# Value rows fetched in turn with key rows inside the GLA recurrences, and narrow products side by side in four lanes, in an fp32 two-layer decoder step

## What is computed

```python
for li in range(DEPTH):                                       # DEPTH = 2
    mod = silu(c) @ ada_w[li] + ada_b[li]                     # 9 rows, 6 kinds of 1024 columns
    sh1, sc1, gt1, sh2, sc2, gt2 = split(mod, 6)
    hm = rmsnorm(x, norm1_g[li]) * (1 + sc1) + sh1
    out, S = rwkv7_mix(hm, ...) if li % 2 == 0 else gla_mix(hm, ...)
    x = x + gt1 * out
    hc = rmsnorm(x, norm2_g[li]) * (1 + sc2) + sh2
    x = x + gt2 * peer(hc, wq[li], subkeys[li], u[li], v[li])

def peer(x, wq, subkeys, u, v):
    # 8 heads, 16 of 128 x 128 experts each by product keys: 128 experts for every token
    expert, gate = top16_of_pairs(x @ wq, subkeys)
    act = gelu(einsum('thed,td->the', u[expert], x))          # key rows: 128 dot products a token
    return einsum('the,thed->td', gate * act, v[expert])      # value rows, weighted
```

## Time and profile before

| | |
|---|---|
| runs of the kernel | 3150.2, 3168.51, 3175.33 us; median 3168.51 |
| the profiled execution | 3167.07 us, its span in the trace 3165.2 us |
| mean granted clock of TensorE | 0.764 of full speed |
| PE busy | 1890.7 us (60 %) |
| DVE busy | 1640.9 us (52 %) |
| POOL busy | 1284.7 us (41 %) |
| PE weight loads | 1084.3 us (34 %, beside PE) |
| ACT busy | 266.3 us (8 %) |
| DMA | 827.99 MB, mean 262 GB/s |

### The profile page before, as it was taken

How to read it: one execution, slowest core, us unless ns; L and a number is a source line. 1 busy time by engine, 2 the same in 40 slices (tenths; PEclk the granted TensorE clock), 3 DMA queues, 4 the chain that set the end, 5 groups by cost and what they waited for, 6 DMA issues and landing times.

```text
span 3165.2 us, 24264 instructions
## 1 busy us (share of the span) xinstructions
PE 1890.7 (60%) x8947; PEld 1084.3 (34%) x8947; DVE 1640.9 (52%) x3013; ACT 266.3 (8%) x421; POOL 1284.7 (41%) x1160
## 2 busy tenths in 40 slices
PE   4889777836947554545684765766346954002537
PEld 1459422326825123333252325343243810000103
DVE  3253375574935437859413226866873262784033
ACT  0111000110100100000100100001110000000000
POOL 0000002452614554535322444466530255777773
PEclk8889888966878776657787877878567967556668
DMA  7530576963858885757887889798775588999996
GB/s 241 175 112 12 194 269 208 344 221 106 269 203 292 331 294 194 243 167 228 286 307 282 307 281 328 249 341 312 225 242 190 218 282 306 380 361 384 409 409 263
DMA packets 296705, 827.99 MB, mean 262 GB/s; under 512 B 45950, under 2 KB 57134, under 8 KB 296588
## 3 DMA queue, kind: packets, MB, share of 16 engines
q0 software_dynamic: 165888, 604.05, 53.1%
q1 hardware_dynamic: 120132, 218.02, 19.9%
q10 hardware_dynamic: 10568, 4.38, 0.5%
HBM read 816.05 MB, written 10.31 MB: 261 GB/s over the span
## 4 chain that ended last, share of the span: by engine, by line
PE 33%; DVE 23%; DMA 19%; POOL 13%; issue 7%; ACT 2%; PEld 1%; SPq 1%; ACTq 0%; DVEq 0%; PEldq 0%; POOLq 0%
PE psum L1750 31%; POOL arena L613 13%; DMA arena<-in_peer_v,idx_v 7%; DVE arena L973 7%; DVE arena L956 7%; DMA wring<-in_gla_w_in 2%; DMA wring<-in_rw_w_rkv 2%; DMA vring<-mod_d 2%; DMA wring<-in_ada_w 1%; DMA wring<-in_peer_wq 1%; DVE hc L956 1%; PE psum L1760 1%; DMA out<-arena 1%; DVE hT L956 1%; PEld psum L1750 1%
## 5 line engine op out<-in xcount | busy, mean ns | idle before, releaser
L1750 PE MATMUL psum<-arena 128*32 128x512 f32 (+6 forms) x4066 | 839.6, 623 | 620.4 <-DMA arena<-in_peer_v,idx_v 279.6
L613 POOL DMA_INDIRECT arena<-in_peer_u,idx_u x576 | 719.5, 1249 | 1094.5 <-DVE acts L973 503.1
L973 DVE CUSTOM_DVE_ANT_0 arena<-arena,hc 128x1024 f32<-128x1024 f32 x576 | 688.7, 1224 | 288.4 <-DMA arena<-in_peer_u,idx_u 219.8
L613 POOL DMA_INDIRECT arena<-in_peer_v,idx_v x512 | 498.8, 974 | 705.0 <-PE psum L1750 551.6
L1750 PEld LDWEIGHTS psum<-arena 128*128 128x128 f32 (+2 forms) x4066 | 399.7, 179 | 1007.9 <-issue 723.7
L1750 PE MATMUL psum<-hT,wring 128*128 128x128 f32 (+3 forms) x1824 | 233.3, 290 | 12.1 <-ACT arena L654 6.3
L1750 PEld LDWEIGHTS psum<-hT,wring 128*128 128x128 f32 (+1 forms) x1824 | 222.0, 195 | 34.8 <-issue 17.1
L1750 PE MATMUL psum<-wring,hT 128*128 128x512 f32 (+1 forms) x480 | 191.7, 559 | 25.1 <-DMA wring<-in_gla_w_in 13.3
L654 ACT ACTIVATE arena<-psum 128x512 f32<-128x512 f32 (+5 forms) x142 | 108.1, 761 | 1131.0 <-PE psum L1750 923.9
L1750 PE MATMUL psum<-wring,cT 128*9 128x512 f32 x384 | 178.1, 622 | 23.0 <-DMA wring<-in_ada_w 16.1
L1750 PE MATMUL psum<-wring,arena 128*128 128x512 f32 (+2 forms) x408 | 157.4, 543 | 26.6 <-DMA wring<-in_rw_w_rkv 13.3
(11 more groups left out here) (207 smaller groups left out, 1564.8 us busy)
## 6 DMA issues: line engine op xcount, KB each, us to landing
wring<-in_ada_w SPq DMA_DIRECT2D x24, 2048.0 KB
wring<-in_peer_wq SPq DMA_DIRECT2D x20, 2048.0 KB
wring<-in_rw_w_rkv SPq DMA_DIRECT2D x12, 2048.0 KB
wring<-in_gla_w_in SPq DMA_DIRECT2D x12, 2048.0 KB
wring<-in_rw_wo SPq DMA_DIRECT2D x6, 2048.0 KB
vring<-mod_d SPq DMA_DIRECT2D x22, 512.0 KB
arena<-in_peer_u,idx_u POOLq DMA_INDIRECT x576, 6.2
arena<-in_peer_v,idx_v POOLq DMA_INDIRECT x512, 6.3
```

Source lines behind the costliest of these rows:

```text
L613: pool.indirect_dma_start(slots[s], None, v_rows if side else u_rows, bass.IndirectOffsetOnAxis(index, 0)).then_inc(rows_landed[s], 16)
L973: dve.tensor_tensor_reduce(slots[s], slots[s], hc[:, t, :], 1.0, 0.0, MUL, ADD, acts[:, (3 * li + t) % 2, col:col + 1]).then_inc(rows_used ...
L1750: return nc.tensor.matmul(out, lhsT, rhs, start=start, stop=stop)
```

## The change

Three parts.

1. **Mingled rounds.** For the one pair in `MINGLED`, layer 2's tile 0, the second half of the key rounds (16 to 31) and the first half of the value rounds (0 to 15) alternate, in `round_at` as in POOL's issue order: one group of the ring then holds key rows, the other value rows. POOL waits for `experts_dealt` after the first key round of the second half. PE opens 16 value rounds ahead of the recurrences of tiles 1 and 2 with a rate of 0.6, multiplies what is left of them behind (`rest_values`), and opens the other 16 where all 32 were opened. On both engines these streams are `paired`: they are served at PSUM results that DVE takes (`for_vector`, `fill`) and at no other wait. DVE's rate goes from 1.6 to 2.4.
2. **The sample tile's values in lanes.** Each of the four slots of a round gets a 32-column product into its own 32 partitions, as for the prompt tiles. One diagonal build takes the place of four. Before the sum is used, DVE copies `total` to SBUF and PE adds the four lanes by a product with `rep32` (`sum_lanes`); this stands once ahead of layer 2's first mixer and once at the end.
3. **Modulations in lanes.** `cT` gets 32 columns for each block (zeros behind the nine), and the eight blocks go to four lanes, two into each. ACT copies the lanes' parts out of PSUM over the first two blocks of the second weight buffer, and PE sums the lanes by a product with nine columns of `rep32`. That buffer is released after this sum.

```diff
--- before.py
+++ after.py
...
-def span_of(t):
-    return 8 if t == SAMPLE else 32
+def spans_of(t):
+    return fetches_of(t) // FOLD
+def spans_ahead(li, t):
+    return sum(spans_of(u) for u in (0, 1, SAMPLE)) * li + sum(spans_of(u) for u in range(t))
+MINGLED = ((1, 0),)
...
     each = fetches_of(t) // GRP
-    return li * 2 * (2 * P + SHORT) // GRP + t * 2 * P // GRP + side * each + r
+    at = side * each + r
+    if (li, t) in MINGLED:
+        first = each // 2
+        if side == 0 and r >= first:
+            at = first + 2 * (r - first)
+        elif side and r < first:
+            at = first + 2 * r + 1
+    return li * 2 * (2 * P + SHORT) // GRP + t * 2 * P // GRP + at
...
     def __init__(self):
-        self.credit, self.rate, self.left = 0.0, 0.0, 0
-    def open(self, count, rate):
+        self.credit, self.rate, self.left, self.paired = 0.0, 0.0, 0, False
+    def open(self, count, rate, paired=False):
...
         self.credit = 0.0
-    def due(self, work):
+        self.paired = paired
+    def due(self, work, product):
+        if self.paired and not product:
+            return 0
...
-        bias_slot, pack_buffer = {}, {}
+        bias_slot, parts_buffer, pack_buffer = {}, {}, {}
+        def parts_of(b):
+            return wring[:, b, 0:2, :].rearrange("p k n -> p (k n)")
...
                 for j in range(2 * k, 2 * k + 2):
-                    weight(a["ada_w"][li][:, j * 512:(j + 1) * 512])
+                    parts_buffer[li, k] = weight(a["ada_w"][li][:, j * 512:(j + 1) * 512])
...
                     rounds = fetches_of(t) // GRP
+                    mingled = (li, t) in MINGLED
...
                         gather(li, t, 0, r)
-                    if t < SAMPLE:
+                        if mingled and r >= rounds // 2:
+                            if r == rounds // 2:
+                                pool.wait_ge(experts_dealt, w.next(experts_dealt))
+                            gather(li, t, 1, r - rounds // 2)
+                    if t < SAMPLE and not mingled:
                         pool.wait_ge(experts_dealt, w.next(experts_dealt))
-                    for r in range(rounds):
+                    for r in range(rounds // 2 if mingled else 0, rounds):
...
                 copy_out(HT(t), D)
+            def copy_parts(li, k):
+                copy_out(parts_of(parts_buffer[li, k]), D)
+                act.sem_inc(parts_copied, 1)
+            def copy_early_parts(li, k):
+                act.wait_ge(mods_parted, w.next(mods_parted))
+                done(act.activation(parts_of(parts_buffer[li, k]), total, ACT.Copy))
+                act.sem_inc(parts_copied, 1)
...
                 root(s16[:, 0, :])
+                for li, k in PREP_MODS[t]:
+                    copy_parts(li, k)
...
                 for li, k in END_MODS[t]:
+                    copy_parts(li, k)
+                for li, k in END_MODS[t]:
...
                     for m in (CHOOSE_MODS[2 * half:2 * half + 2] if first else ()):
+                        copy_early_parts(*m)
...
                 if first:
+                    copy_early_parts(*CHOOSE_MODS[4])
...
             act.sem_inc(operand_written, 1)
-            copy_out(cT[:, :], KD * 9)
+            copy_out(cT[:, :].rearrange("p (k n) -> p k n", k=KD)[:, :, 0:9], KD * 9)
...
             copy_out(muT[:, :], 48)
+            for k in range(2):
+                copy_parts(0, k)
...
             stream = Share()
-            RATES = {"mix": 14, "core1": 1.9, "core2": 2.6, "enter": 6, "gla": 1.6, "out": 7}
+            RATES = {"mix": 14, "core1": 1.9, "core2": 2.6, "enter": 6, "gla": 2.4, "out": 7}
...
-            def open_rows(li, t, first, count, rate):
+            def open_rows(li, t, first, count, rate, paired=False):
                 at[:] = li, t, first
-                stream.open(count, rate)
-            def serve(work=1.0):
-                for _ in range(stream.due(work)):
+                stream.open(count, rate, paired)
+            def serve(work=1.0, product=False):
+                for _ in range(stream.due(work, product)):
...
             def fill():
-                serve()
+                serve(1.0, True)
...
                     dve.wait_ge(total_ready, phase)
-                span = span_of(t)
-                m = D // span
+                span, m = FOLD, D // FOLD
                 src = (acts if t == SAMPLE else wf)[:, phase % 2, :]
-                for q in (range(4) if t == SAMPLE else (2 * half, 2 * half + 1)):
+                for q in ((0,) if t == SAMPLE else (2 * half, 2 * half + 1)):
...
                 dve.wait_ge(total_ready, 3 * li + t + 1)
+                if t == SAMPLE:
+                    done(dve.tensor_copy(tmp, total))
+                    dve.sem_inc(lanes_copied, 1)
+                    dve.wait_ge(lanes_summed, w.next(lanes_summed))
...
                     weights_due(1, 0, 0)
-                    open_rows(1, 0, 64, 64, RATES["gla"])
+                    open_rows(1, 0, 64, 64, RATES["gla"], True)
...
             at = [0, 0, 0]
-            VALUE_RATES = {"out": 0.5, "gla": 0.5}
+            VALUE_RATES = {"out": 0.5, "gla": 0.5, "mingled": 0.6, "core2": 0.8}
...
                 at[2] += 1
-                phase, span, rounds = 3 * li + t, span_of(t), fetches_of(t) // GRP
+                phase, span, rounds = 3 * li + t, FOLD, fetches_of(t) // GRP
...
                 if r * GRP % span == 0:
-                    pe.wait_ge(diag_ready, 4 * phase + chunk + 1)
+                    pe.wait_ge(diag_ready, spans_ahead(li, t) + chunk + 1)
...
                     for j in range(GRP):
-                        lane = slice(0, P) if t == SAMPLE else slice(m * j, m * j + m)
-                        start = r == 0 and (j == 0 or t != SAMPLE)
-                        stop = r == rounds - 1 and (j == GRP - 1 or t != SAMPLE)
+                        lane = slice(m * j, m * j + m)
+                        start, stop = r == 0, r == rounds - 1
...
-            def open_values(li, t, rate):
-                at[:] = li, t, 0
-                stream.open(fetches_of(t) // GRP, rate)
+            def sum_lanes():
+                pe.wait_ge(lanes_copied, w.next(lanes_copied))
+                for h in range(2):
+                    last = mm(total[:, h * 512:(h + 1) * 512], rep32[:], add_tmp[:, h * 512:(h + 1) * 512])
+                last.then_inc(lanes_summed, 1)
+            def open_values(li, t, rate, count=None, first=0, paired=False):
+                at[:] = li, t, first
+                stream.open(fetches_of(t) // GRP if count is None else count, rate, paired)
...
-            def serve(work=1.0):
-                for _ in range(stream.due(work)):
+            def serve(work=1.0, product=False):
+                for _ in range(stream.due(work, product)):
...
             def for_vector():
-                serve()
+                serve(1.0, True)
...
-            def modulation():
-                ps = for_vector()
+            def mod_parts(dst):
...
                     for kk in range(KD):
-                        last = mm(ps[0:9, j * 512:(j + 1) * 512], cT[:, kk * 9:(kk + 1) * 9], wring[:, b, kk, :], kk == 0, kk == KD - 1)
+                        g = FOLD * (kk % COPIES)
+                        last = mm(dst[g:g + FOLD, j * 512:(j + 1) * 512], cT[:, kk * FOLD:(kk + 1) * FOLD],
+                                  wring[:, b, kk, :], kk < COPIES, kk >= COPIES)
...
                         last.then_inc(weight_used[b], 1)
-                    else:
-                        last.then_inc(psum_for_vector, 1)
-                        release(b, psum_for_vector, nfv[0])
+                return last, b
+            def mod_sum(dst, b):
+                pe.wait_ge(parts_copied, w.next(parts_copied))
+                for j in range(2):
+                    last = mm(dst[0:9, j * 512:(j + 1) * 512], rep32[:, 0:9], parts_of(b)[:, j * 512:(j + 1) * 512])
+                return last
+            def modulation():
+                last, b = mod_parts(for_scalar())
+                last.then_inc(psum_for_scalar, 1)
+                mod_sum(for_vector(), b).then_inc(psum_for_vector, 1)
+                release(b, psum_for_vector, nfv[0])
...
                     pe.wait_ge(mods_taken, n)
-                for j in range(2):
-                    b = weight()
-                    for kk in range(KD):
-                        last = mm(total[0:9, j * 512:(j + 1) * 512], cT[:, kk * 9:(kk + 1) * 9], wring[:, b, kk, :], kk == 0, kk == KD - 1)
-                    if j == 0:
-                        last.then_inc(weight_used[b], 1)
-                    else:
-                        last.then_inc(mods_summed, 1)
-                        release(b, mods_summed, n + 1)
+                last, b = mod_parts(total)
+                last.then_inc(mods_parted, 1)
+                mod_sum(total, b).then_inc(mods_summed, 1)
+                release(b, mods_summed, n + 1)
...
+                if tiles[0]:
+                    sum_lanes()
...
```

(5 more changed lines are left out.)

8 lines of the change are left out of this document (7 added, 1 removed).

## The result

The changed kernel takes 3115.01 us (median of four runs, 3103.15 to 3122.44) against 3167.65 us for the kernel before: the ratio is 0.9848, with a 95 % interval of 0.9813 to 0.9884. The forecast was 3101 us. The profiled execution took 3103.15 us with a span of 3101.3 us, so the trace shows a gain of 63.9 us of span where the medians show 52.6: it is the quickest of the four.

The account below looks back on a forecast made before the run. No engine was taken to bound the kernel: a chain of stages in series. 3165.2 less 21 (mingled rounds), 16 (sample lanes) and 29 (modulations), plus 0.5, gave 3099.7, so 3101 us; range 3065 to 3145 for 8 in 10.

Parts of the forecast that it names:

- the second rival: Lower clock and loads: PE's short modulation bursts run at 3.64 us, that part is worth 12, time 3118 us; chance 0.14.
- 65 us of growth: Recurrences of layer 2's tiles 1 and 2: 16 added value rounds lengthen them by 65 us.
- 86.5 us of the stages behind: Behind the recurrences: sample tile's choice ends at 2618.5, so next key products start 86.5 us sooner than at 2705.0.
- The ten distances: Ten of fifteen distances between mingled value rounds, paced by a slot group's trip of 14.2 us: 142 us together.
- the five longer ones: Five distances between mingled value rounds set by the recurrence's own work: 85.9 us now, 91.4 with the added rounds.
- its floor: Mingled value rounds: a group's trip (slots freed, gathers issued, landing, round) of 14.2 us is their least distance.
- S: What the recurrences of layer 2's tiles 1 and 2 grow by: 65 us taken, about 45 to 100 as bounds.
- The price of POOL's issue: Gathers in the recurrences: 1.32 us each and some 0.3 between them, adding 1.2 us to a group's trip.
- land the last 5.7 us later: Sample tile's end: after POOL issues the 16 gathers left in 19 us, the last value rows land 5.7 us later.
- the 35 to 38 of the sign: Sign of being right: the sample tile's last eight value rounds take 35 to 38 us.
- Three places: Modulations at the start, ahead of the first recurrence and in the first choice: gains of 7, 7.4 and 10 us.
- the 5 us taken there: Modulations at the sample tile's end, paced by two loads at once: gain between 3 and 7.5 us, 5 taken.

Follow-up runs that it names:

- the kernel without a way out: The whole change, but modulations leave out ACT's copy and PE's sum, so only the first lane's blocks reach the result: ratio 0.9829 to the kernel before.

## Why the prediction was right, and where its terms were off

**The range and the sign** held: 3115 lies in 3065 to 3145, and all three parts gain. The forecast's own band, 3088 to 3112, was missed by 3 us. The time is nearer to the second rival's 3118 than to 3101, but by another sum: that rival took 17 us from the modulations alone, while the runs take 5 to 7 us from each of the three parts.

**Mingled rounds: the sizes right, by a mechanism that holds where the value side is last.** Forecast were 65 us of growth and 86.5 us of the stages behind; measured 63 to 69, and 79 to 81. The second was short by the second deal: the prediction let PE's rounds end long ahead of it, but with PE at 3.3 us a round and 6.4 to 7.3 us from start to start the last ends at 2622.4, and the deal comes 6 to 8 us sooner instead of 13.6.

The first can be taken apart in the change's trace. The ten distances that the prediction set at 142 us together take 144.2, the five longer ones, set at 91.4, take 86.6. Eight of the ten are closed trips of 13.9 us for the 14.2, with parts that were off against each other: from the first to the fourth issue 3.9 us for 4.9, from there to PE's start 6.4 for 5.7, the round 3.4 for 3.64. Value rounds do have a pace of their own, and the rates don't set it: 15.4 us on average, and 15.3 with rates a quarter higher. What the prediction lacks is how close the key side stands behind: shortening the trip frees 13 us where its floor would free 20 or 26, and fewer value rounds free 0 to 8. That S came within 2 us is in part luck: the ten distances came out 2 us longer and the five 5 us shorter.

The price of POOL's issue was the part read too high. It came from a window in which DVE was full; in the same 69 us of the changed stage POOL is busy 39.5 us for 35 gathers, 1.13 each where the earlier trace rows had 1.32, and DVE is idle a third of the time.

```profile
2158.37:2227.37 69.00, 26.70 (x132) 13.38 (x136) 45.27 (x77) 10.36 (x19) 39.45 (x35) 0.60 0.74 251
```

**Sample tile's lanes: the term was mis-sized, 9 us for 16.** The step that failed is "land the last 5.7 us later": that landing came from a stretch with a short queue. At the end four gathers of 128 rows take 5.1 us because the DMA is full, and the rounds wait for them: from the last issue to PE's start it is 12.8 us, 7.1 more than the 5.7, and POOL, which waits for the rounds, issues its last gather 4 us later than the sum had it. The queue was noticed and given 5 us; it cost 11.4 more than the first sum, and the rounds take 43.0 us, not the 35 to 38 of the sign. Copy and sum were right: 5.2 for 4.6. In layer 1 the builds win 4.1 to 4.3 us and the way from there to the sum's use loses 5.7, in the trace of this part alone and in the change's: about 1.5 us lost for the half that was forecast.

**Modulations' lanes: 22 us for 29, in part by accident.** Three places measured 4.1, 6.0 and 7.2 us for 7, 7.4 and 10. Over the ten kernels with lanes and sum, against the three without lanes, they are 6.4, 4.3 and 6.4. The rows say why:

```profile
34.05 3.12 PE L1809 MATMUL psum<-wring,cT 128*32 128x512 f32 x16 [2.31 <-DMA wring<-in_ada_w]
...
39.98 3.64 PE L1809 MATMUL psum<-wring,cT 128*32 128x512 f32 x16 [2.82 <-DMA wring<-in_ada_w]
...
467.90 3.47 PE L1809 MATMUL psum<-wring,cT 128*32 128x512 f32 x16 [1.12 <-DMA wring<-in_ada_w]
474.23 2.98 PE L1809 MATMUL psum<-wring,cT 128*32 128x512 f32 x16 [2.86 <-DMA wring<-in_ada_w]
```

```profile
177.97 1.21 DVE L1005 TENSOR_TENSOR vring<-psum,vring 9x1024 f32<-9x1024 f32 x1 [1.77 <-PE psum L1809]
...
465.86 1.21 DVE L1005 TENSOR_TENSOR vring<-psum,vring 9x1024 f32<-9x1024 f32 x1 [0.43 <-DVE idx_u L1601]
482.08 1.21 DVE L1005 TENSOR_TENSOR vring<-psum,vring 9x1024 f32<-9x1024 f32 x1 [13.44 <-PE psum L1809]
```

Halves now wait for weights, and behind such a wait ten of eleven take 3.0 to 3.6 us, near the 3.64 of the lower clock (1.2 GHz), not 1.92; in the trace of this part alone it is eight of twelve. This is the second rival's step in part, and the Trainium skill's rule in TensorE: Matmul & The Clock Gate, section "HAM oscillation — how this bites in real kernels"; the trace agrees for most halves behind a wait, while the five that followed other work at once took 1.9. In the first choice DVE becomes late by itself at 465.86 (0.43 us idle), and behind it the last modulation's halves wait for their weights. At the sample tile's end loads pace, and the 5 us taken there are nothing: the ten kernels lead by 26.7 us ahead of it and by 25.9 behind it.

Something else helps, which no sum had. In lanes a modulation opens two PSUM results, one for ACT and one for DVE, where it opened one, and PE's stream of layer 1's value rounds is served at each. So a value round now stands between the two modulations at the sample tile's end, and DVE waits less for the last round of that tile. PE after; then DVE's addition of that sum before, after, and in the kernel without a way out, which opens one result again:

```profile
1523.28 1.92 PE L1809 MATMUL psum<-arena 128*32 128x512 f32 x16 [0.41 <-PE psum L1809]
```

```profile
1886.41 1.22 DVE L956 TENSOR_TENSOR arena<-psum,vring 128x1024 f32<-128x1024 f32 x1 [21.65 <-PEq L1695]
```

```profile
1847.90 1.22 DVE L1005 TENSOR_TENSOR arena<-psum,vring 128x1024 f32<-128x1024 f32 x1 [17.91 <-PEq L1747]
```

```profile
1855.90 1.22 DVE L997 TENSOR_TENSOR arena<-psum,vring 128x1024 f32<-128x1024 f32 x1 [21.12 <-PEq L1739]
```

The wait is 17.0 to 18.3 us in the ten kernels, all of which have this round, and 21.1 to 23.1 in the four that open one result, none of which has it. From the second of these modulations to this addition it takes 310.3 us on average in the ten and 318.1 in the four. So about 8 us of what the lanes are worth come from one more place where a shared stream is served. The kernel without a way out loses them.

**What stays open.** At the weighing at 2193 us ten kernels with modulations in lanes lead the three without by 32.6 us on average (2161.4 against 2194.0). The three places are 17.1 of it and the accident some 8; the rest builds up in small steps between the first choice and the sample tile's end, none of them at a modulation, and has no cause shown. Yet the runs of that part alone show 21.8. Its own trace loses 12.7 us behind that point: 2.8 in the recurrences, 3.2 up to the addition of tile 0's sum, and 6.7 in the 460 us behind it, where the DMA is nearly full (share 0.94). Why isn't known. And with the change's 0.9848 come 48 us, not the profiled 63.9: that execution is early by 9.7 us at 2150 already, against the mean of the nine others.

Two of the prediction's sums are off by a little, without effect on the outcome: 39.1 with a slow half and the sum is 46.0, not 45.5, and 2 us more in each of fifteen trips make S 95, not 100.

## What to carry to other kernels

A price for a landing or for a gather's issue holds only for the queue that it was read from: before it is moved, look at the DMA's share in the stage where it will stand. When two streams share one issuing engine and one ring, each side's waits reach the other through the issue order; a floor worked out for one side holds only where that side is last, and the other may stand close behind. Count in how many distances the trip is closed, and try it by shortening one part at a time. When a small product becomes quick, its weights' loads and its way out of PSUM are late next, and both can be read beforehand. An edit that adds a wait or a result also adds a place where shared streams are served, and so moves work that it doesn't name.

## What the runs showed of the hardware

Sixteen products of 32 columns, four side by side, take 1.92 us at the full clock (2.4 GHz) for what sixteen of 9 columns took 7.03 us before: a gain of 3.7 in fp32. With the DMA queue full, gathers of 128 rows of 4 KB land one in 1.28 us, 410 GB/s, all issued by POOL, and PE starts 12.8 us behind the last issue; with rows of 2 KB POOL's issue of 1.25 us becomes the bound. In the recurrences, where the DMA share of the change is 0.74 in the first 69 us, it is 6.8 us from the last issue to PE's start with rows of 4 KB and 4.8 with rows of 2 KB. A gather's issue costs POOL 1.13 us of busy time on average in the changed stage, and 1.32 in the stage before, where DVE was full.
